# Every other residual add of an entry moved from VectorE to GpSimd

## The chip, the cores and the metric

The kernel runs on one core of a Trainium2 chip. The metric is the device time of one execution in microseconds (us), the median over runs. An execution has TensorE (PE, with its weight loads PEld), VectorE (DVE), ScalarE (ACT), GpSimd (POOL), and SyncE (SP), which starts the transfers.

## The reference

A first block (gated delta rule, windowed attention, a merge) works on 512 tokens of width 1024, and two transformer layers follow. The change touches only how one sublayer hands over to the next in these layers. There the reference does the following, four times a layer:

```
f = swiglu(rmsnorm(h, g[0]), ffn_gate[i, 0], ffn_up[i, 0], ffn_down[i, 0])
h = h + MACARON * rmsnorm(f, g[1])
mix = hybrid_mixer(rmsnorm(h, g[2]), ...)
h = h + rmsnorm(mix, g[3])
...
gate = jax.nn.sigmoid(rmsnorm(h, g[6]) @ w_ple_gate[i])
h = h + rmsnorm((p[i] @ w_ple[i]) * gate, g[7])
```

That is: norm the output of one sublayer, add it to the residual `h`, norm the residual, and multiply it by the first weights of the next sublayer.

## The kernel before

The residual lies in SBUF as `[128, 8, 512]`: 8 tiles (`KD`) of 128 features by 512 tokens, float32. Products are made of split numbers: a value is a rounded part `hi` and a remainder `lo`, and `matmul3` (L224 to L229) makes three matmuls, hi by hi, lo by hi, hi by lo. Weights arrive in granules of 128x1024, of which ScalarE makes `w_hi` (L181) and VectorE `w_lo` (L189).

A sublayer ends in an `Exit`, which gathers the sum of squares of its output (GpSimd adds the squared tiles, L508; TensorE sums over features, L515 and L518; ScalarE takes the root, L481; VectorE its reciprocal, L500). The next one begins with an `Entry`, which works in two halves of 256 tokens. For each half and each tile t:

- scale (VectorE, L331): output tile times its gain times the reciprocal root, into one of four buffers
- add (VectorE, L336): the residual tile plus that buffer
- h_hi and the square (ScalarE, L357 and L360), h_hi being the residual tile times a gain, rounded
- rest (VectorE, L340): the remainder `h_lo`
- products (TensorE, L227 to L229 out of `pe_products`) for the first two weight granules, and a sum of the square (L376)

The norm's own reciprocal root is applied to the products later, so TensorE can start as soon as tile 0 has its h_lo. Each engine runs its own list in order, and semaphores join them. VectorE's list for a half is written in steps s = 0, 1, ...: scale of tile s, add of tile s - 1, rest of tile s - 3, and then what `make` puts in (a weight split, or in Ffn 0 of layer 1 the late parts of the sublayer before). TensorE goes through the tiles of half 0, then those of half 1. Ahead of each half VectorE takes the reciprocal of the sublayer before.

Each layer has four entries: Ffn 0, MixIn, Ffn 1 (after MixOut) and Ple. The first Ffn has no sublayer before it (`leave` is None) and does no scale or add. The other seven entries do both. `chain` (L582) gives every engine the lists of the sublayers one behind the other.

Of the kernel before, what the change touches and what calls it, by code (L numbers as in the profile page):

```python
# [22 lines left out]
ALU = mybir.AluOpType  # L23
# [5 lines left out]
KD = D // P  # L29
# [55 lines left out]
class Mark:  # L85


    def __init__(self, sem, base):
        self.sem, self.base = sem, base
# [214 lines left out]
def cols(half):  # L304
    return slice(half * HALF, (half + 1) * HALF)


class Entry:
# [6 lines left out]
    def __init__(self, kit, g0, gain, delta_gain, leave):  # L315
        self.kit, self.g0, self.gain, self.delta_gain, self.leave = kit, g0, gain, delta_gain, leave
        self.hi, self.lo = kit.h
        self.buf, self.sq = (kit.work[:, a:a + 2].rearrange("p a (b n) -> p (a b) n", b=2) for a in (0, 2))
        n = 2 * KD
        self.scaled, self.added = kit.mark("scaled", n if leave else 0), kit.mark("added", n if leave else 0)  # L320
        self.rounded, self.h_ready = kit.mark("rounded", n), kit.mark("h_ready", n)
        self.squared, self.summed = kit.mark("squared", n), kit.mark("summed", n)
        self.rooted, self.rstd_ready = kit.mark("rooted", 2), kit.mark("rstd_ready", 2)

    def dve_half(self, dve, half, make=None):
        kit, x, c, at = self.kit, self.kit.residual, cols(half), half * KD

        def scale(t):
            if at + t >= 4:
                dve.wait_ge(*self.added(at + t - 3))  # L330
            dve.scalar_tensor_tensor(self.buf[:, (at + t) % 4], self.leave.source(t, half), self.delta_gain(t),  # L331
                                     kit.rstd[:, c], ALU.mult, ALU.mult).then_inc(self.scaled.sem, 1)

        def add(t):
            dve.wait_ge(*self.scaled(at + t + 1))
            dve.tensor_tensor(x[:, t, c], x[:, t, c], self.buf[:, (at + t) % 4], ALU.add).then_inc(self.added.sem, 1)  # L336

        def rest(t):
            dve.wait_ge(*self.rounded(at + t + 1))
            dve.scalar_tensor_tensor(self.lo[:, t, c], x[:, t, c], self.gain(t), self.hi[:, t, c].bitcast(F32), ALU.mult,  # L340
                                     ALU.subtract).then_inc(self.h_ready.sem, 1)

        for s in range(KD + 3):
            if self.leave and s < KD:
                scale(s)
            if self.leave and 1 <= s <= KD:
                add(s - 1)
            if s >= 3:
                rest(s - 3)
            if make:  # L350
                make(s)

    def act_tile(self, act, half, t):
        x, c, n = self.kit.residual, cols(half), half * KD + t
        if self.leave:
            act.wait_ge(*self.added(n + 1))
        act.activation(self.hi[:, t, c], x[:, t, c], ACT.Copy, scale=self.gain(t)).then_inc(self.rounded.sem, 1)  # L357
        if n >= 4:
            act.wait_ge(*self.summed(n - 3))
        act.activation(self.sq[:, n % 4], x[:, t, c], ACT.Square).then_inc(self.squared.sem, 1)  # L360
# [92 lines left out]
class Exit:  # L453
# [49 lines left out]
    def pool(self, pool):  # L503
        for t in range(1, self.full):
            pool.wait_ge(*self.out_squared(t + 1))
            if t >= 2:
                pool.wait_ge(*self.out_added(t - 1))
            pool.tensor_tensor(self.total, self.total, self.sq[:, t % 2], ALU.add).then_inc(self.out_added.sem, 1)  # L508
# [19 lines left out]
class Last:  # L528
# [26 lines left out]
    def pool(self, pool):  # L555
        pass
# [25 lines left out]
def chain(kit, sublayers):  # L582

    with stage(kit) as (block, _):
        @block.sync
        def _(sp):
            for s in sublayers:
                s.sp(sp)

        @block.tensor  # L590
        def _(pe):
            for s in sublayers:
                s.pe(pe)

        @block.gpsimd
        def _(pool):
            for s in sublayers:
                s.pool(pool)

        @block.scalar  # L600
        def _(act):
            for s in sublayers:
                s.act(act)

        @block.vector
        def _(dve):
            for s in sublayers:
                s.dve(dve)
# [1453 lines left out]
class Ffn:  # L2062
# [23 lines left out]
        fetch_ahead(self.kit, sp, self.g0, self.GRANULES)  # L2086

    def pool(self, pool):
        self.exit.pool(pool)

    def pe(self, pe):
# [120 lines left out]
class MixIn:  # L2212
# [21 lines left out]
        sp.wait_ge(*self.loaded(16 * len(self.loads)))  # L2234

    def pool(self, pool):
        pass

    def pe(self, pe):
        kit, g0, h = self.kit, self.g0, self.kit.h  # L2240
# [302 lines left out]
class Ple:  # L2543
# [19 lines left out]
        fetch_ahead(self.kit, sp, self.e0, 3 + KD)  # L2563

    def pool(self, pool):
        self.exit.pool(pool)

    def pe(self, pe):
# [433 lines left out]
```

## Time and profile before

| | |
|---|---|
| median of 3 runs | 3286.45 us (3285.54 to 3293.07) |
| profiled execution, its time | 3287.4 us |
| profiled execution, its span | 3285.6 us |
| mean granted TensorE clock | 0.961 |
| TensorE, VectorE, ScalarE, GpSimd busy | 91%, 48%, 36%, 9% |

The span goes from the first to the last instruction. The granted clock is a share of TensorE's full 2.4 GHz; 0.5 is 1.2 GHz. A busy share is an average over stages in which different engines are the limit. The places around the change are short: one entry takes some 30 us.

### The profile page before, as it was taken

The numbers are of one execution on the slowest core, as the hardware profiler recorded it, in microseconds if no ns is written. First come the engines' busy times: TensorE is split into PE (matmuls) and PEld (weight loads), VectorE is DVE, ScalarE is ACT, GpSimd is POOL, SyncE is SP. The second block draws the span as 40 slices with busy tenths as digits, with TensorE's granted clock in tenths as the row PEclk, the third lists the DMA queues.
The fourth block names the chain that finished last, engine by engine and source line by source line (L and its number), as shares of the span: only waits on it lengthen the run. The fifth ranks groups of instructions, "written<-read, shape, count | busy, mean of one in ns | idle before, by whom it ended". The sixth has DMA issues, their size and how long they took to land. (4 is left out here: it accounts for less than half of the span.)

```text
span 3285.6 us, 39993 instructions
## 1 busy us (share of the span) xinstructions
PE 2989.3 (91%) x15628; PEld 2500.4 (76%) x15628; DVE 1591.2 (48%) x2721; ACT 1193.1 (36%) x2017; POOL 294.9 (9%) x273
## 2 busy tenths in 40 slices
PE   5988799887999999959899999899999778999997
PEld 2877699866778888837688888788888556888886
DVE  5725465433454434356464434654435375644336
ACT  4324544233242223136442323533223345432234
POOL 0001086600000000020000000000000010000000
PEclk8999899999999999989999999999999899999998
DMA  5220100022223332210222332233332101232321
GB/s 211 71 70 1 63 1 1 1 65 68 85 90 97 96 103 84 90 39 1 65 83 97 96 103 84 64 110 96 99 106 84 58 1 39 77 96 97 102 92 57
DMA packets 66858, 241.93 MB, mean 74 GB/s; under 512 B 7408, under 2 KB 9584, under 8 KB 66032
## 3 DMA queue, kind: packets, MB, share of 16 engines
q1 hardware_dynamic: 66672, 239.38, 22.5%
q8 instruction: 125, 2.05, 0.3%
q14 instruction: 61, 0.50, 0.1%
HBM read 236.21 MB, written 3.15 MB: 73 GB/s over the span
## 5 line engine op out<-in xcount | busy, mean ns | idle before, releaser
L227 PE MATMUL pair<-h_hi_at,w_hi_at 128*128 128x512 f32 (+1 forms) x2048 | 781.8, 382 | 45.9 <-DVE h_lo_at L340 30.6
L228 PE MATMUL pair<-h_lo_at,w_hi_at 128*128 128x512 f32 (+1 forms) x2048 | 760.6, 371 | 0.0
L229 PE MATMUL pair<-h_hi_at,w_lo_at 128*128 128x512 f32 (+1 forms) x2048 | 760.5, 371 | 0.0
L189 DVE TENSOR_TENSOR w_lo_at<-w_raw,w_hi_at 128x1024 fp32r<-128x1024 f32 x350 | 437.0, 1251 | 472.8 <-ACT w_hi_at L181 472.7
L181 ACT ACTIVATE w_hi_at<-w_raw 128x1024 fp32r<-128x1024 f32 x350 | 366.0, 1052 | 537.8 <-PE pair L229 521.6
L227 PEld LDWEIGHTS pair<-h_hi_at,w_hi_at 128*128 128x128 f32 x2048 | 389.8, 190 | 121.7 <-DVE h_lo_at L340 37.0
L228 PEld LDWEIGHTS pair<-h_lo_at,w_hi_at 128*128 128x128 f32 x2048 | 390.1, 190 | 67.2
L229 PEld LDWEIGHTS pair<-h_hi_at,w_lo_at 128*128 128x128 f32 x2048 | 390.1, 190 | 65.8
L2181 DVE TENSOR_TENSOR work_at<-pair,rstd_at 128x512 f32<-128x512 f32 (+1 forms) x184 | 122.2, 668 | 363.2 <-PE pair L229 363.1
L227 PE MATMUL pair<-a_hi_at,w_hi_at 128*128 128x512 f32 (+1 forms) x792 | 290.1, 366 | 0.0
L228 PE MATMUL pair<-a_lo_at,w_hi_at 128*128 128x512 f32 (+1 forms) x792 | 289.4, 365 | 0.0
L229 PE MATMUL pair<-a_hi_at,w_lo_at 128*128 128x512 f32 (+1 forms) x792 | 289.4, 365 | 0.0
L508 POOL TENSOR_TENSOR exit_work_at<-exit_work_at 128x512 f32<-128x512 f32 x44 | 57.9, 1315 | 2161.6 <-ACT exit_work_at L470 2161.4
L227 PE MATMUL pair<-h_hi,w_hi 128*128 128x512 f32 (+1 forms) x432 | 166.8, 386 | 28.7 <-DVE h_lo L264 21.1
L2157 ACT ACTIVATE work_at<-work_at 128x512 f32<-128x512 f32 x88 | 55.6, 632 | 334.7 <-DVE work_at L2181 334.7
L228 PEld LDWEIGHTS pair<-a_lo_at,w_hi_at 128*128 128x128 f32 x792 | 149.3, 189 | 24.5
L227 PEld LDWEIGHTS pair<-a_hi_at,w_hi_at 128*128 128x128 f32 x792 | 149.4, 189 | 24.2
L229 PEld LDWEIGHTS pair<-a_hi_at,w_lo_at 128*128 128x128 f32 x792 | 149.3, 189 | 23.9
L228 PE MATMUL pair<-h_lo,w_hi 128*128 128x512 f32 (+1 forms) x432 | 164.0, 380 | 0.0
L229 PE MATMUL pair<-h_hi,w_lo 128*128 128x512 f32 (+1 forms) x432 | 163.7, 379 | 0.0
L189 DVE TENSOR_TENSOR w_lo<-w_raw,w_hi 128x1024 fp32r<-128x1024 f32 x59 | 71.9, 1224 | 185.2 <-ACT w_hi L181 185.2
L181 ACT ACTIVATE w_hi<-w_raw 128x1024 fp32r<-128x1024 f32 x59 | 62.1, 1059 | 216.1 <-PE pair L229 195.7
(394 smaller groups left out, 4353.9 us busy)
## 6 DMA issues: line engine op xcount, KB each, us to landing
w_raw<-in_weights SPq DMA_DIRECT2D x433, 512.0 KB, 3.5
residual<-in_x SPq DMA_DIRECT2D x1, 2048.0 KB, 12.4
cos_sin_at<-rope_table SPq DMA_DIRECT2D x2, 1024.0 KB, 4.7
out<-residual SPq DMA_DIRECT2D x16, 128.0 KB, 1.7
ctx_in<-in_ctx SPq DMA_DIRECT2D x1, 1024.0 KB, 13.0
rope_table<-zb SPq DMA_DIRECT2D x1, 1024.0 KB, 4.9
mask_at<-in_layer_masks SPq DMA_DIRECT2D x2, 512.0 KB, 4.7
levels<-in_levels SPq DMA_DIRECT2D x1, 896.0 KB, 8.3
```

The costliest lines, as they stand in the source:

```text
L181: eng.activation(self.w_hi[:, g % self.split].rearrange("p k n -> p (k n)"), self.w_raw[:, slot], ACT.Copy).then_inc(self.w_hi_ready, 1)
L189: eng.tensor_tensor(self.w_lo[:, g % self.split].rearrange("p k n -> p (k n)"), self.w_raw[:, g % RAW], self.w_hi[:, g % self.split].rearr ...
L227: pe.matmul(out, sh, mh, start=start, stop=False)
L228: pe.matmul(out, sh, ml, start=False, stop=False)
L229: return pe.matmul(out, sl, mh, start=False, stop=stop)
L508: pool.tensor_tensor(self.total, self.total, self.sq[:, t % 2], ALU.add).then_inc(self.out_added.sem, 1)
L2157: act.activation(self.gate[:, f % 2], self.gate[:, f % 2], ACT.Silu).then_inc(self.gate_silu.sem, 1)
L2181: last = dve.tensor_tensor(dst[:, f % 2, c], bank, kit.rstd[:, c], ALU.mult)
```

## The change

Adds of even tiles stay on VectorE. Adds of odd tiles go to GpSimd, whose list gets an entry's adds ahead of its exit's. The one semaphore `added` becomes two, one for each engine. Tile n is ready when the semaphore n % 2 has counted n // 2 + 1, so `added(n)` now takes the number of a tile where it took a count. What is computed stays the same. The entry of Ffn, MixIn and Ple is changed; `Last`, the final adds, is not.

```diff
-        self.scaled, self.added = kit.mark("scaled", n if leave else 0), kit.mark("added", n if leave else 0)
+        self.scaled = kit.mark("scaled", n if leave else 0)
+        self.added_by = [kit.mark(x, KD if leave else 0) for x in ("added_by_dve", "added_by_pool")]
...
+    def added(self, n):
+
+        return self.added_by[n % 2](n // 2 + 1)
+
+    def add(self, eng, half, t):
+        x, c, n = self.kit.residual, cols(half), half * KD + t
+        eng.wait_ge(*self.scaled(n + 1))
+        eng.tensor_tensor(x[:, t, c], x[:, t, c], self.buf[:, n % 4], ALU.add).then_inc(self.added_by[n % 2].sem, 1)
+
+    def pool(self, pool):
+        if self.leave:
+            for half in range(2):
+                for t in range(1, KD, 2):
+                    self.add(pool, half, t)
+
     def dve_half(self, dve, half, make=None):
...
             if at + t >= 4:
-                dve.wait_ge(*self.added(at + t - 3))
+                dve.wait_ge(*self.added(at + t - 4))
...
-        def add(t):
-            dve.wait_ge(*self.scaled(at + t + 1))
-            dve.tensor_tensor(x[:, t, c], x[:, t, c], self.buf[:, (at + t) % 4], ALU.add).then_inc(self.added.sem, 1)
...
             if self.leave and 1 <= s <= KD:
-                add(s - 1)
+                if s % 2:
+                    self.add(dve, half, s - 1)
...
     def act_tile(self, act, half, t):
...
-            act.wait_ge(*self.added(n + 1))
+            act.wait_ge(*self.added(n))
...
     def pool(self, pool):
+        self.entry.pool(pool)
         self.exit.pool(pool)
```

The last edit stands in Ffn and Ple; in MixIn, which has no exit of its own, `pass` becomes `self.entry.pool(pool)`.

## Rows read from the trace of the kernel before

**Rows 1.** The page's busy time, share of the span and instructions.
```profile
PE 2989.3 (91%) x15628; PEld 2500.4 (76%) x15628; DVE 1591.2 (48%) x2721; ACT 1193.1 (36%) x2017; POOL 294.9 (9%) x273
L227 PE MATMUL pair<-h_hi_at,w_hi_at 128*128 128x512 f32 (+1 forms) x2048 | 781.8, 382 | 45.9 <-DVE h_lo_at L340 30.6
```

**Rows 2.** Timeline of TensorE: start, duration, instruction, idle before and releaser.
```profile
2837.36 0.39 PE L227 MATMUL pair<-h_hi_at,w_hi_at 128*128 128x256 f32 x1 [2.15 <-DVE h_lo_at L340]
...
2841.86 0.43 PE L227 MATMUL pair<-h_hi_at,w_hi_at 128*128 128x256 f32 x1
...
2822.91 0.39 PE L227 MATMUL pair<-h_hi_at,w_hi_at 128*128 128x256 f32 x1 [3.31 <-DVE h_lo_at L340]
...
1295.56 0.39 PE L227 MATMUL pair<-h_hi_at,w_hi_at 128*128 128x256 f32 x1 [0.50 <-DVE h_lo_at L340]
...
2111.91 0.39 PE L227 MATMUL pair<-h_hi_at,w_hi_at 128*128 128x256 f32 x1 [2.19 <-DVE h_lo_at L340]
...
2037.02 0.38 PE L227 MATMUL pair<-h_hi_at,w_hi_at 128*128 128x256 f32 x1 [1.65 <-DVE w_lo_at L189]
```

**Rows 3.** One line's instructions, L336: duration min/median/max ns, first and last start.
```profile
L336 DVE TENSOR_TENSOR residual<-residual,work_at x112: 411/420/426, 1292.1 to 3223.5; 128x256 f32<-128x256 f32 x112
```

**Rows 4.** Timeline of VectorE in half 1 of Ffn 1, layer 1.
```profile
2834.23 0.88 DVE L331 SCALAR_TENSOR_TENSOR work_at<-delta_at,small,rstd_at 128x256 f32<-128x256 f32 x2
2835.03 0.42 DVE L336 TENSOR_TENSOR residual<-residual,work_at 128x256 f32<-128x256 f32 x1
2835.36 0.48 DVE L331 SCALAR_TENSOR_TENSOR work_at<-delta_at,small,rstd_at 128x256 f32<-128x256 f32 x1
2835.76 0.42 DVE L336 TENSOR_TENSOR residual<-residual,work_at 128x256 f32<-128x256 f32 x1
...
2836.83 0.48 DVE L340 SCALAR_TENSOR_TENSOR h_lo_at<-residual,small,h_hi_at 128x256 fp32r<-128x256 f32 x1
...
2841.33 0.48 DVE L340 SCALAR_TENSOR_TENSOR h_lo_at<-residual,small,h_hi_at 128x256 fp32r<-128x256 f32 x1
```

**Rows 5.** Timeline of the rope stage, and L2200, a 128x512 VectorE multiply elsewhere.
```profile
1443.99 1.27 POOL L1174 TENSOR_TENSOR by_cos_at<-qh_at,cos_sin_at 128x512 f32<-128x512 f32 x1 [0.63 <-DVE k_rope_at L1197]
...
1444.55 1.26 DVE L1197 TENSOR_TENSOR qh_at<-by_cos_at,by_sin_at 128x512 f32<-128x512 f32 x1
...
L2200 DVE TENSOR_TENSOR work_at<-work_at x88: 692/693/693, 955.5 to 3076.5; 128x512 f32<-128x512 f32 x88
```

**Rows 6.** Timeline at the end of Ple, layer 1.
```profile
3259.64 0.41 DVE L2691 TENSOR_TENSOR delta_at<-emb_at,sig_at 128x256 f32<-128x256 f32 x1
3259.76 1.45 POOL L508 TENSOR_TENSOR exit_work_at<-exit_work_at 128x512 f32<-128x512 f32 x1
...
3260.21 1.28 DVE L2691 TENSOR_TENSOR delta_at<-emb_at,sig_at 128x256 f32<-128x256 f32 x1 [0.15 <-ACT sig_at L2675]
```

**Rows 7.** Timeline in the delta rule's inversion stage.
```profile
429.74 0.43 DVE L1637 TENSOR_SCALAR inv_a<-inv_low 128x512 f32<-128x512 f32 x1
429.77 1.53 POOL L1721 TENSOR_TENSOR inv_b<-inv_a,levels 128x512 f32<-128x512 f32 x1
...
430.08 1.50 DVE L1638 TENSOR_SCALAR inv_low<-inv_low 128x512 f32<-128x512 f32 x1
```

**Rows 8.** Small and one-sided GpSimd instructions, by line.
```profile
L1310 POOL COPY scores<-small x32: 185/185/187, 263.2 to 343.9; 128x1 f32<-128x1 f32 x32
...
L879 POOL MEMSET c_wide<- x1: 312/312/312, 0.8 to 0.8; 128x256 f32 x1
...
L1763 POOL MEMSET scan_state<- x2: 525/525/525, 607.3 to 607.8; 128x512 f32 x2
```

**Rows 9.** Stretches: length, busy time (x instructions), granted clock, DMA share, GB/s.
```profile
2822.91:2826.60 3.69, 3.69 (x15) 3.51 (x16) 3.69 (x11) 2.16 (x7) 0.00 (x0) 0.54 0.02 4
...
2111.91:2122.94 11.03, 10.88 (x64) 10.14 (x65) 6.15 (x16) 4.90 (x13) 0.00 (x0) 0.85 0.00 0
1308.40:1317.87 9.47, 9.31 (x65) 8.57 (x65) 6.06 (x16) 5.05 (x13) 0.00 (x0) 1.00 0.00 0
```

More of the change, by code:

```diff
@@ L2236, in pool @@
     def pool(self, pool):
-        pass
+        self.entry.pool(pool)
     def pe(self, pe):
@@ L2565, in pool @@
     def pool(self, pool):
+        self.entry.pool(pool)
         self.exit.pool(pool)
```

## The prediction

> **What bounds the kernel now.** I read the page first. TensorE is busy 91% of the span, VectorE 48%, GpSimd 9% [rows 1]. So VectorE work costs time only where TensorE waits for it. The groups of instructions then say where: the idle time ahead of products of h is put down to `h_lo` of L340, the last VectorE step of an entry. The timeline shows those waits one by one [rows 2]: the reader is to see that TensorE idles 2.15 us at the start of half 1 of an entry, 3.31 us at the start of half 0 after an attention output (Ffn 1), but 0.50 us in half 0 of MixIn. In Ple it waits 1.65 us for a weight split (L189), not for h.
>
> Seven entries have a `leave`: MixIn and Ffn 1 of both layers, Ple of both, and Ffn 0 of layer 1. 112 adds of 0.42 us stand in them [rows 3], 16 an entry; 56 go to GpSimd.
>
> Then I read VectorE's order in half 1 of Ffn 1, layer 1 [rows 4]. Each instruction starts 0.08 us before the last one ends, so a scale or a rest costs 0.40 us of the stream and an add 0.34. The first rest ends at 2837.31 and TensorE starts at 2837.36 [rows 2]. The rest of tile 4 ends at 2841.81 and its products start at 2841.86: up to tile 4 TensorE runs at VectorE's pace of 1.13 us a tile. Behind that TensorE sets the pace itself.
>
> **What is taken away.** Four adds a half, 0.34 us each. Two halves of waiting would give back one add ahead of the first rest in each, 0.68 us an entry, if GpSimd's adds ran beside VectorE for nothing.
>
> **What comes in their place.** Whether they run beside each other is what decides, and three places of the trace show that they don't.
> - In the rope stage VectorE adds two SBUF tensors of 128x512 while GpSimd multiplies. GpSimd ends at 1445.26, VectorE at 1445.81, 1.26 us after its start; the same shape with GpSimd quiet takes 0.69 [rows 5]. VectorE's work began when GpSimd's was over and took 0.55 more.
> - With 128x256, our shape: GpSimd ends at 3261.21 and VectorE's multiply at 3261.49, 0.28 later, 1.28 us after its start in place of 0.41. In the same rows the first multiply ends at 3260.05, and GpSimd, which had started at 3259.76, ends 1.16 later; its instruction alone takes 1.27. So GpSimd waits too, and 0.14 us of its instruction lie ahead of the part that excludes the other engine [rows 6].
> - VectorE's next instruction doesn't get in first. At 429.74 and 430.08 two stand back to back; GpSimd starts at 429.77, ends 1.14 after the first, at 431.30, and only then does the second finish, at 431.58 [rows 7]. Whoever asks first goes first. These two read one tensor each; ours read two, as in rows 5 and 6.
>
> All VectorE instructions around the new adds (scale, add, rest) read two SBUF tensors, except the two scales that read PSUM.
>
> The Trainium skill says this too ("SBUF — State Buffer", SBUF: two separate sides): VectorE with two SBUF inputs and GpSimd reading SBUF take one port pair exclusively, the first holding it for a whole instruction. By that rule the change costs time; the rows above agree, so it is my sum and not a separate rival.
>
> **The price of a GpSimd add of 128x256.** No row has it. Two inputs at 128x512 take 1.27 us [rows 5]; a copy of one element takes 0.185 [rows 8]. Half the elements: 0.185 + (1.27 - 0.185) / 2 = 0.73 us. The memsets (0.53 for 512, 0.31 for 256) scale alike. Bounds: below, 0.31, a memset of this shape that reads nothing; above, 1.27, as if half a tile cost what a whole one does. I take 0.73, since every pair of sizes here scales so, and 0.59 of it excludes VectorE. The VectorE instruction behind it then ends 0.28 (an add) or 0.34 (scale, rest: 0.48 against 0.42) later. One collision thus puts 0.59 + 0.34 - 0.40 = 0.53 us into the stream, for an add that took 0.34.
>
> The Trainium skill ("GPSIMD Engine Reference", Performance versus the Vector engine) gives 4.50 us for a float add of 2048 elements. In proportion that is an estimate of 0.56 us for 256; with it the sum below would be about 3 us in place of 8.
>
> **One half, step by step** (half 1 of Ffn 1, from [rows 4]). The second scale ends at 2835.11; GpSimd's add of tile 1 starts 0.08 later, at 2835.19, as in rows 5, and asks at 2835.33. VectorE's add of tile 0 ends at 2835.45, so GpSimd ends at 2836.04 and scale 2 (started 2835.37) at 2836.38. Scale 3 ends 2836.78, add 2 at 2837.12. GpSimd's add of tile 3 asks at 2837.00, ahead of rest 0 (started 2837.04, asks about 2837.18), and ends at 2837.71; rest 0 ends at 2838.05, not 2837.31: 0.74 late. Two collisions, one add saved. Rest 1 has another add saved and is 0.42 late. Each further pair of tiles has one collision and one saved add. Rest 4 has four collisions against three saved adds: 4 x 0.53 - 3 x 0.34 = 1.10; followed out to the instruction it is 1.18. Since TensorE takes tile 4 as soon as it is ready, half 1 ends 1.18 us late.
>
> In half 0 it depends on the entry. Ffn 1 starts from idle: TensorE is 0.74 late at tile 0 and keeps it, since at nearly half clock [rows 9] its products are then slower than VectorE's pace. In MixIn it is TensorE again from tile 2, so rest 1's 0.42 stays (the weight split behind add 0 collides as scale 2 does). In Ffn 0 of layer 1 two VectorE instructions that read PSUM follow add 0 (L2684); GpSimd's first add runs beside them, and one collision less one add, 0.2, stays. Everything between the halves hangs on TensorE's sum through ScalarE's root, so half 1 starts late by the same.
>
> ScalarE's waits cost nothing: GpSimd's tile 1 is ready at 2836.04, before ScalarE has done with tile 0. The scales' waits for `added(n-4)` are long met. GpSimd's queue holds only the adds of the exits, which end before the entry's first scale or begin after its last tile.
>
> Sum: MixIn 2 x (0.42 + 1.18) = 3.2; Ffn 1 2 x (0.74 + 1.18) = 3.8; Ffn 0 0.2 + 0.74 = 0.9 (its half 1 is already slow by the clock, next part, so only the first wait counts); Ple 2 x 0.2 = 0.4, since its half 0 lies beside other products. Together 8.3 us.
>
> **The clock.** Half 1 of Ffn 0 takes 11.03 us at a mean granted clock of 0.85, half 1 of MixIn 9.47 at 1.00 [rows 9]. Both began after nearly the same idle, 2.19 and 2.16. So these waits stand at the edge: four of five kept 2.4 GHz, while the 3.31 us ahead of Ffn 1's half 0 was followed by 0.54, nearly all at 1.2 GHz [rows 9], and even the 1.65 in Ple has such a stretch behind it. The change lengthens the wait of 2.15 to 2.15 + 0.74 = 2.9. I take it that three of the four fall. Each costs 11.03 - 9.47 = 1.56, less the 1.18 - 0.74 = 0.44 by which VectorE's delay then hides behind the slower products: 1.1 us, together 3.4.
>
> 8.3 + 3.4 = 11.7. The profiled execution took 3287.4 (span 3285.6), 0.95 over the median of 3286.45; from the median that gives 3298.
>
> **The rivals.** A measurement here tells a change from none at about 0.3%, 9.9 us.
> - A, the forecast: exclusion and most waits over the clock's edge, +11.7, 3298. Chance 0.42.
> - B, exclusion, the clock holds: +8.3, 3294.8, within 0.3%. For it: four of five waits held so far. Against it: 2.9 is much nearer to 3.31. 0.30.
> - C, GpSimd's adds run beside VectorE: 0.68 us back in each of the five entries, -3.4, 3283. This is the one on the other side. It decides where a collision costs less than 0.34 us, a GpSimd add under 0.54. Against it all of rows 5 to 7. 0.08.
> - D, a GpSimd half tile costs nearly a whole one: each collision 1.08 us, rest 4 late by 3.3, an entry by about 5; with five, +25, 3311. Against it the memsets. 0.12.
> - E, VectorE's next instruction always goes first: one collision fewer ahead of each rest, 0.2 and 0.6 an entry, +4, 3290. Against it rows 7. 0.08.
>
> Range 3289 to 3305: it takes in A, B and E, and part of the way to D. Slower by over 0.3%: A and D, less those of A in which only one or two waits fall, 0.50. Within 0.3%: B, C, E and that part, 0.46. Faster, 0.04.
>
> **What would show it.** Right: GpSimd adds recorded at 0.73 to 0.9 us; scales and rests behind them at 0.9 to 1.1 in place of 0.48; TensorE's wait ahead of half 1 near 2.9; the granted clock of more half 1 stretches below 1. Wrong: rests that keep 0.48 (C), waits of 2.9 with the clock at 1.00 (B), GpSimd adds above 1.2 (D).

## The result and the profile after

| | before | after |
|---|---|---|
| median of 21 runs each, us | 3287.59 (3285.34 to 3293.29) | 3295.79 (3293.30 to 3299.64) |
| profiled execution, us | 3287.4 | 3294.15 |
| its span, us | 3285.6 | 3292.4 |
| mean granted TensorE clock | 0.961 | 0.960 |

The ratio is 1.0023, with a 95% interval of 1.0016 to 1.0030: slower beyond its interval, by less than the 0.3% named in the prediction. The medians are 8.2 us apart, the profiled spans 6.8. The kernel before is here 1.1 us above the 3286.45 from which the forecast was counted, so 8.2 is to be compared with its +11.7.

The page's busy times and the group of TensorE that waits for `h_lo` (us busy, mean ns | idle before; L352 is the rest, which was L340):

```profile
PE 2992.8 (91%) x15628; PEld 2503.3 (76%) x15628; DVE 1600.0 (49%) x2665; ACT 1191.2 (36%) x2017; POOL 342.0 (10%) x329
...
L227 PE MATMUL pair<-h_hi_at,w_hi_at 128*128 128x512 f32 (+1 forms) x2048 | 782.7, 382 | 50.7 <-DVE h_lo_at L352 36.4
```

Beside [rows 1], VectorE does 56 instructions fewer and is busy 9 us longer. The idle time put down to `h_lo` has grown from 30.6 to 36.4 us. The adds themselves, one line for both engines (ns, shortest/median/longest):

```profile
L333 DVE TENSOR_TENSOR residual<-residual,work_at x56: 407/414/422, 1291.3 to 3229.9; 128x256 f32<-128x256 f32 x56
L333 POOL TENSOR_TENSOR residual<-residual,work_at x56: 833/846/858, 1291.4 to 3230.1; 128x256 f32<-128x256 f32 x56
```

Now half 1 of Ffn 1, layer 1, the stretch of [rows 4]. First VectorE's timeline (start, duration, instruction), then GpSimd's and TensorE's in the same stretch. The third row is a pair of scales, and the fourth repeats the second of that pair, from a narrower window.

```profile
2840.51 0.88 DVE L347 SCALAR_TENSOR_TENSOR work_at<-delta_at,small,rstd_at 128x256 f32<-128x256 f32 x2
2841.31 0.42 DVE L333 TENSOR_TENSOR residual<-residual,work_at 128x256 f32<-128x256 f32 x1
2841.65 1.34 DVE L347 SCALAR_TENSOR_TENSOR work_at<-delta_at,small,rstd_at 128x256 f32<-128x256 f32 x2
2842.51 0.47 DVE L347 SCALAR_TENSOR_TENSOR work_at<-delta_at,small,rstd_at 128x256 f32<-128x256 f32 x1
2842.91 0.41 DVE L333 TENSOR_TENSOR residual<-residual,work_at 128x256 f32<-128x256 f32 x1
2843.24 0.94 DVE L352 SCALAR_TENSOR_TENSOR h_lo_at<-residual,small,h_hi_at 128x256 fp32r<-128x256 f32 x1
...
2848.03 0.95 DVE L352 SCALAR_TENSOR_TENSOR h_lo_at<-residual,small,h_hi_at 128x256 fp32r<-128x256 f32 x1
```

```profile
2841.47 0.83 POOL L333 TENSOR_TENSOR residual<-residual,work_at 128x256 f32<-128x256 f32 x1 [7.66 <-DVE work_at L347]
2843.07 0.84 POOL L333 TENSOR_TENSOR residual<-residual,work_at 128x256 f32<-128x256 f32 x1 [0.76 <-DVE work_at L347]
```

```profile
2844.24 0.38 PE L227 MATMUL pair<-h_hi_at,w_hi_at 128*128 128x256 f32 x1 [2.76 <-DVE h_lo_at L352]
```

What to see: VectorE's add ends at 2841.73. GpSimd's add, started at 2841.47, ends 0.58 us behind it, at 2842.31 (the rows cut thousandths off). VectorE's next scale starts at 2841.65 and ends 0.28 behind GpSimd, at 2842.59 (the pair's 1.34 us less the second scale's own part): 0.94 us for an instruction that takes 0.48 in [rows 4]. The rest meets GpSimd's second add in the same way and takes 0.94. Such a meeting is called a collision below. All 56 adds of GpSimd end 0.58 to 0.60 us (median 0.59) behind the VectorE add that they met, and a scale or rest that has waited for one ends 0.28 behind it. In one place nothing has to wait: behind VectorE's first add in Ffn 0 of layer 1 stand two VectorE instructions that read PSUM (L2684 before), and they keep their 0.75 us beside GpSimd's add:

```profile
2097.01 0.75 DVE L2699 TENSOR_TENSOR sig_at<-pair,rstd_at 128x256 f32<-128x256 f32 x2
```

```profile
2096.84 0.84 POOL L333 TENSOR_TENSOR residual<-residual,work_at 128x256 f32<-128x256 f32 x1 [5.70 <-DVE work_at L347]
```

Back in Ffn 1, it is 3.67 us from the first scale's start to the end of rest 0 where [rows 4] has 3.08, so rest 0 is 0.59 late and TensorE waits 2.76 in place of 2.15 [rows 2]. Rest 4 ends 8.47 after the first scale in place of 7.58: 0.89 late.

The same differences, read for each entry, with the time at which half 1's reciprocal root comes and the end of the entry, both against before and from the entry's first scale on (the rests of half 1 from its own reciprocal on):

| entry | rest 0 late, half 0 | half 1's reciprocal late | rest 0, rest 4 late, half 1 | end of entry late |
|---|---|---|---|---|
| MixIn, layer 0 and 1 | 0.68 | 0.34, 0.36 | 0.60, 0.88 | 2.29, 1.88 |
| Ffn 1, layer 0 and 1 | 0.60 | 0.45, 0.41 | 0.60, 0.89 | 1.31, 1.28 |
| Ffn 0, layer 1 | 0.13 | 1.10 | 0.60, 0.88 | 0.38 |
| Ple, layer 0 and 1 | 0.70 | 0.03, 0.02 | 0.59, 0.88; 0.23, 0.52 | 0.03, -0.37 |

The ends add to 6.80 us, the difference between the spans. Outside the entries the differences cancel (0.8 us earlier ahead of the first, 0.9 later between MixIn and Ffn 1 of layer 0, 0.1 earlier later on).

MixIn's first rest is 0.68 late and not 0.60 because its first collision falls on the weight split of L189, which takes 1.76 us in place of 1.22. One number of the table is not the change's: the 1.10 of Ffn 0. Its rests 1 to 4 of half 0 are not late at all. TensorE ran its half 0 at 1.2 GHz for longer, 5.7 us in place of 3.6 behind its first product, and the kernels half1_only and early_half1 below, whose half 0 is that of before, show 1.13 and 1.08 at the same place.

The clock in the stretches of half 1, in the order MixIn 0, Ffn 1 of layer 0, Ffn 0, MixIn 1, Ffn 1 of layer 1 (length, TensorE busy, granted clock, DMA share, GB/s):

```profile
1308.53:1319.35 10.82, 10.82 (x64) 0.84 0.00 0
1663.21:1672.93 9.72, 9.52 (x64) 1.00 0.01 2
2117.34:2127.05 9.71, 9.51 (x64) 1.00 0.00 0
2491.60:2501.98 10.38, 10.38 (x64) 0.86 0.00 0
2844.24:2853.95 9.71, 9.50 (x64) 1.00 0.01 2
```

Both MixIn stretches, which had 1.00 before, contain a part at 1.2 GHz. Both of Ffn 1 do not, behind the same wait. Ffn 0's, the one at 0.85 in [rows 9], is now at 1.00, though its wait grew from 2.19 to 2.79:

```profile
2117.34 0.39 PE L227 MATMUL pair<-h_hi_at,w_hi_at 128*128 128x256 f32 x1 [2.79 <-DVE h_lo_at L352]
...
2491.60 0.58 PE L227 MATMUL pair<-h_hi_at,w_hi_at 128*128 128x256 f32 x1 [2.76 <-DVE h_lo_at L352]
```

### The profile page after: what moved, and what is told of

It is laid out like the page before. It is cut to its first block and busy times, and to the rows that moved or that the text cites. A ratio compares the mean times of both kernels' runs of the same rounds, so it can differ in the third digit from the quotient of the medians.

```text
span 3292.4 us, 39993 instructions
## 1 busy us (share of the span) xinstructions
PE 2992.8 (91%) x15628; PEld 2503.3 (76%) x15628; DVE 1600.0 (49%) x2665; ACT 1191.2 (36%) x2017; POOL 342.0 (10%) x329
## 5 line engine op out<-in xcount | busy, mean ns | idle before, releaser
L227 PE MATMUL pair<-h_hi_at,w_hi_at 128*128 128x512 f32 (+1 forms) x2048 | 782.7, 382 | 50.7 <-DVE h_lo_at L352 36.4
L189 DVE TENSOR_TENSOR w_lo_at<-w_raw,w_hi_at 128x1024 fp32r<-128x1024 f32 x350 | 439.2, 1257 | 471.7 <-ACT w_hi_at L181 471.6
L189 DVE TENSOR_TENSOR w_lo<-w_raw,w_hi 128x1024 fp32r<-128x1024 f32 x59 | 71.9, 1224 | 184.7 <-ACT w_hi L181 184.6
```

Of the source, the lines that this page charges most:

```text
L189: eng.tensor_tensor(self.w_lo[:, g % self.split].rearrange("p k n -> p (k n)"), self.w_raw[:, g % RAW], self.w_hi[:, g % self.split].rearr ...
L227: pe.matmul(out, sh, mh, start=start, stop=False)
```

## The experiments

Ratios are to the kernel before, timed on the same chip, with 95% intervals; "late" is against the profiled execution of before, in half 1 from its own reciprocal on. In the first four, VectorE keeps all 16 adds of an entry, and GpSimd in addition works on spare tiles at the moments at which the change would have it add: work that nothing reads.

**beside_add: the added cost alone, nothing taken from VectorE**

```diff
+    def pool(self, pool):
+        if self.leave:
+            for n in range(1, 2 * KD, 2):
+                pool.wait_ge(*self.scaled(n + 1))
+                pool.wait_ge(*self.beside(n // 2))
+                pool.tensor_tensor(self.kit.squares[:, 5:7], self.kit.squares[:, 7:9], self.kit.squares[:, 0:2], ALU.add).then_inc(self.beside.sem, 1)
```

> All residual adds stay on VectorE, as in the kernel before. GpSimd, at the moments at which the change has it add a tile, adds two constant 128x256 tiles into a place that nobody reads, and no engine waits for it. Theory 1 (exclusion: the two engines take turns): the changed kernel showed its first rest 0.60 us late with two collisions and one add saved, so a collision is (0.60 + 0.34) / 2 = 0.47 us; with no add saved the first rest of half 1 is 0.94 late, the rest of tile 4 is 1.9 late, MixIn and Ffn 1 lose 2.8 us each, Ffn 0 2.3, together +13 us (3300), and a scale behind such an add takes 0.95 us in place of 0.48. Theory 2 (the cost is that GpSimd hands its tiles over late): nobody waits for these adds, so no rest is late and the time stays at the 3287 of before.

3307.95 us (4 executions), ratio 1.0056 (1.0041 to 1.0071). VectorE in half 1 of Ffn 1, layer 1, then GpSimd:

```profile
2854.68 0.88 DVE L339 SCALAR_TENSOR_TENSOR work_at<-delta_at,small,rstd_at 128x256 f32<-128x256 f32 x2
2855.47 0.42 DVE L344 TENSOR_TENSOR residual<-residual,work_at 128x256 f32<-128x256 f32 x1
2855.81 0.95 DVE L339 SCALAR_TENSOR_TENSOR work_at<-delta_at,small,rstd_at 128x256 f32<-128x256 f32 x1
...
2857.74 0.95 DVE L348 SCALAR_TENSOR_TENSOR h_lo_at<-residual,small,h_hi_at 128x256 fp32r<-128x256 f32 x1
```

```profile
2855.64 0.84 POOL L331 TENSOR_TENSOR squares<-squares 128x256 f32<-128x256 f32 x1 [7.67 <-DVE work_at L339]
2857.57 0.84 POOL L331 TENSOR_TENSOR squares<-squares 128x256 f32<-128x256 f32 x1 [1.09 <-DVE work_at L339]
```

Two VectorE instructions ahead of the end of rest 0 take 0.95 in place of 0.48, and that rest is 0.94 late: two collisions of 0.47. Rest 4, behind four, is 1.88 late, 0.47 each. With the change's saved adds (0.34 each) taken off, 2 x 0.47 - 0.34 = 0.60 and 4 x 0.47 - 3 x 0.34 = 0.86, against 0.59 to 0.60 and 0.88 to 0.89 in the change. The addends are constants in tiles of their own, so it is neither the data nor the residual that VectorE waits for. The rests came as Theory 1 has them, the time did not: its sum was +13 us, and the medians are 19.7 apart. The other 6.7 are not shown to be exclusion (in the profiled execution 3.5 had arisen ahead of the first entry, where the kernels don't differ).

**beside_memset: the same moments, an instruction that reads nothing** (the edit is to beside_add)

```diff
-                pool.tensor_tensor(self.kit.squares[:, 5:7], self.kit.squares[:, 7:9], self.kit.squares[:, 0:2], ALU.add)...
+                pool.memset(self.kit.squares[:, 5:7], 0.0)...
```

> As beside_add, but GpSimd's instruction is a memset of 128x256, which reads nothing. Theory 1a (only a GpSimd instruction that reads SBUF excludes VectorE): rests not late, +0 us. Theory 1b (any GpSimd instruction does): a memset of 0.31 us less 0.14 ahead and 0.07 of slack costs 0.10 us a collision, the rest of tile 4 is 0.4 late, +3 us. Theory 2: +0 us.

3294.57 us, ratio 1.0011 (1.0001 to 1.0020). No rest 0 to 4 of any half is late, counted from the half's own reciprocal, and the scales keep their time:

```profile
L331 POOL MEMSET squares<- x56: 311/311/315, 1292.8 to 3230.3; 128x256 f32 x56
...
L339 DVE SCALAR_TENSOR_TENSOR work_at<-delta_at,small,rstd_at x96: 476/482/493, 1291.9 to 3228.7; 128x256 f32<-128x256 f32 x96
```

So the price is not that of GpSimd having something to do, nor of its semaphores. But the time is longer, and the trace puts part of that on the clock. Two stretches, the first and the second MixIn, behind waits of 2.15 us as before:

```profile
1309.00:1318.47 9.47, 9.31 (x65) 1.00 0.00 0
2490.89:2501.97 11.08, 10.92 (x65) 0.85 0.00 0
```

```profile
2490.89 0.39 PE L227 MATMUL pair<-h_hi_at,w_hi_at 128*128 128x256 f32 x1 [2.15 <-DVE h_lo_at L348]
```

The second holds a part at 1.2 GHz and is 1.61 us longer. Half 1 of Ffn 1, layer 0, did the same (its entry ends 2.13 late), and some 4 us of the span's 7.5 arose outside the entries. It bears on every comparison here: two kernels that wait equally long can differ by several us. Why this one is above before in ten executions, and not only in the profiled one, stays open.

**beside_copy and beside_add128: one input (the edit is to beside_memset), and half the size**

```diff
-                pool.memset(self.kit.squares[:, 5:7], 0.0)...
+                pool.tensor_copy(self.kit.squares[:, 5:7], self.kit.squares[:, 7:9])...
```

> As beside_add, but GpSimd copies one 128x256 tile, so it reads one tensor. Theory 1 (one input is enough): a copy of about 0.45 us costs some 0.25 us a collision, the rest of tile 4 is 1.0 late, about +6 us. If only two inputs on both sides exclude: +0. Theory 2: +0.

3296.82 us, ratio 1.0025 (1.0015 to 1.0034).

```profile
L331 POOL COPY squares<-squares x56: 526/533/538, 1294.5 to 3233.4; 128x256 f32<-128x256 f32 x56
```

Rest 0 of half 1 is 0.27 late, rest 4 0.55: 0.14 a collision. The copy takes 0.53 us with its wait, so it costs VectorE less than the 0.25 that I expected; by the medians the kernel is 8.6 us above before all the same, where I expected 6.

The second is beside_add with one tile of 128x128 in place of each 128x256:

```diff
-                pool.tensor_tensor(self.kit.squares[:, 5:7], self.kit.squares[:, 7:9], self.kit.squares[:, 0:2], ALU.add)...
+                pool.tensor_tensor(self.kit.squares[:, 5:6], self.kit.squares[:, 7:8], self.kit.squares[:, 0:1], ALU.add)...
```

> As beside_add with half the width: GpSimd adds two constant 128x128 tiles that nobody waits for. It settles how the price of a collision goes with size. By the line through 0.185 us (one element) and 1.27 us (512) the add takes 0.46 us, excludes VectorE for 0.32, and a collision costs 0.32 + 0.30 - 0.40 = 0.22 us, so the first rest of half 1 is 0.44 late. If the price belongs to the instruction and not its size: 0.94 late as in beside_add. If GpSimd's overhead lies inside the exclusion: about 0.6 late.

A single execution, 3301.19 us.

```profile
L331 POOL TENSOR_TENSOR squares<-squares x56: 565/570/583, 1294.7 to 3237.3; 128x128 f32<-128x128 f32 x56
```

Rest 0 is 0.40 late, rest 4 0.80: 0.20 a collision. With 0.47 at 128x256, half the work on GpSimd costs VectorE 0.27 less. VectorE's own instructions kept their size, so 0.20 and 0.47 differ by GpSimd's half tile alone. It ends 0.32 us behind VectorE's add, as the line through 0.185 and 1.27 has it.

**half1_only, half0_only: the change in one half of each entry**

```diff
+        self.on_pool = [n for n in range(n) if n % 2 and n >= KD]
+        self.on_dve = [n for n in range(2 * KD) if n not in self.on_pool]
...
-                if s % 2:
+                if at + s - 1 in self.on_dve:
                     self.add(dve, half, s - 1)
```

(the diff is to the changed kernel; half0_only has `n < KD`)

> The change in half 1 alone; half 0 keeps all its adds on VectorE. Theory 1: half 0 as before, in half 1 the first rest 0.60 late and the rest of tile 4 0.88, so 0.9 us in each of the five entries where TensorE waits, +4.4 us, and some more where the wait of 2.76 in place of 2.15 makes the clock fall (1.1 and 0.7 us in the two entries in which it fell in the changed kernel). Theory 3 (the changed kernel's cost comes from half 0, and half 1 only inherits it): +0.

> The change in half 0 alone. Theory 1 (a collision costs 0.47 us, a saved add gives 0.34): rest 0 of half 0 is 0.6 late, rest 1 0.27; MixIn carries 0.34 into half 1, Ffn 1 0.4 to 0.6, Ple and Ffn 0 nothing; the wait ahead of half 1 keeps its 2.15 us, and half 1 its length. Together +1.5 to +2 us without the clock, less than a comparison can tell. Theory 3 (the changed kernel's cost comes from half 0): +7.

half1_only: 3294.38 us, ratio 1.0018 (1.0008 to 1.0027). Half 0 is unchanged to 0.01 us up to rest 4; in half 1 rest 0 is 0.60 late and rest 4 0.89, and TensorE waits 2.75 to 2.80. The stretches of half 1 of both MixIn and of Ffn 1, layer 0, hold parts at 1.2 GHz.

half0_only: 3292.54 us, ratio 1.0009 (1.0000 to 1.0018). Rest 0 of half 0 is 0.60 late in Ffn 1 and 0.68 in MixIn, half 1's reciprocal 0.35 late in MixIn and 0.59 and 0.46 in Ffn 1; behind it half 1 is unchanged, with waits of 2.15. Still both MixIn stretches fell, again behind unlengthened waits.

The delays of the rests are those of the whole change, half by half. The times, 0.18% and 0.09% against 0.23% for the whole, agree within their intervals, which are as wide as the smaller part. Ffn 1's reciprocal shows less than it seems: in layer 0 it is 0.35 late in half1_only, whose half 0 is that of before, and 0.94 in beside_memset, where no rest up to tile 4 is late.

**last_only: only tile 7 of each half goes to GpSimd**

```diff
-        self.on_pool = [n for n in range(n) if n % 2 and n >= KD]
+        self.on_pool = [n for n in range(n) if n % KD == 7]
```

> GpSimd adds only tile 7 of each half, the one tile whose add comes after the wait is over. Theory 1: its collision falls ahead of rest 4, which is 0.47 late, while the saved add shows from rest 5 on (0.13 late). So TensorE loses 0.47 in half 1 of the five entries, +2.3 us without the clock. If an add could be moved for nothing once TensorE has its first tile: -0 to -1 us.

3294.40 us, ratio 1.0017 (1.0008 to 1.0026). Rests 0 to 3 are unchanged. Rest 4, which meets the one GpSimd add, is 0.47 late; rest 5, with its saved add, 0.14. Tile 7 is the only add of a half that lies behind all scales and the first rests, and it gains nothing: the price shows on the rest that it meets. In the MixIn of layer 0 the entry ends 0.42 late. MixIn 1 and both Ffn 1 fell in clock, with waits of 2.15 to 2.16 ahead of them, and ended 1.61 to 2.15 late. By the medians it is 5.8 us above before, where the sum without the clock was 2.3.

**early_half1, early_both: VectorE keeps the adds, the rest of a tile comes one step earlier**

If a first rest that is late by 0.6 costs time, one that is early by the same reasoning gives some back. The second scale-and-add pair ahead of rest 0 needs no second engine to get out of its way: rest 0 can stand ahead of it.

```diff
-    def dve_half(self, dve, half, make=None):
+    def dve_half(self, dve, half, make=None, lag=3):
...
-            if s >= 3:
-                rest(s - 3)
+            if lag <= s < KD + lag:
+                rest(s - lag)
...
-        self.dve_half(dve, 1)
+        self.dve_half(dve, 1, lag=2)
```

early_both does it in half 0 too, unless the sublayer before is Ple, and ScalarE takes the earlier sublayer's squares one tile sooner:

```diff
-                if half == 0 and t == 3 and leave:
+                if half == 0 and leave and t == (3 if isinstance(leave, GatedExit) else 2):
                     leave.act_squares(act, 1)
...
-        self.dve_half(dve, 0, make)
+        self.dve_half(dve, 0, make, lag=3 if isinstance(leave, GatedExit) else 2)
```

> All adds on VectorE as before, but in half 1 VectorE does the rest of tile s - 2 in step s in place of s - 3, so that one scale and one add fewer stand ahead of the first rest. If VectorE's order ahead of the first rest is what TensorE waits for, every rest of half 1 up to tile 4 ends 0.73 us earlier, the wait of 2.15 becomes 1.42, and five entries give 3.7 us; the clock may give 1.1 to 1.6 more in the entry where half 1 ran slow. -3.7 to -5. If ScalarE's h_hi is the limit (0.51 us after add 0): nothing.

> As early_half1, and in half 0 too (not where the sublayer before is Ple), with ScalarE's squares of the last output tile one tile earlier, since adds of tile 2 on then come 0.40 later and TensorE's sum would wait for them. Half 0 of MixIn and Ffn 1 gives another 0.73 each: -6.6 us without the clock, 3280 beside a before of 3287. If only one half's wait can be shortened because the other takes it up: no more than early_half1.

> The same kernel as early_both, beside early_both_split on one chip: a ratio to before of 0.9976 within its interval again, and a profiled execution that shows whether the stretches at 1.2 GHz stay at the same entries (they fell in MixIn and Ffn 1 of layer 0) or move from execution to execution.

| | median, us | ratio (interval) |
|---|---|---|
| early_half1 | 3283.68 | 0.9984 (0.9975 to 0.9993) |
| early_both | 3281.25 | 0.9976 (0.9967 to 0.9985) |
| early_both_again, the same kernel | 3281.90 | 0.9982 (0.9973 to 0.9991) |

By the medians these are 4.9, 7.4 and 6.1 us under before, where 3.7 and 6.6 were the sums without the clock; the second comparison bears the first out.

early_both in half 1 of Ffn 1, layer 1; VectorE, then TensorE:

```profile
2837.64 0.42 DVE L336 TENSOR_TENSOR residual<-residual,work_at 128x256 f32<-128x256 f32 x1
2837.98 0.48 DVE L331 SCALAR_TENSOR_TENSOR work_at<-delta_at,small,rstd_at 128x256 f32<-128x256 f32 x1
2838.37 0.42 DVE L336 TENSOR_TENSOR residual<-residual,work_at 128x256 f32<-128x256 f32 x1
2838.71 0.48 DVE L340 SCALAR_TENSOR_TENSOR h_lo_at<-residual,small,h_hi_at 128x256 fp32r<-128x256 f32 x1
```

```profile
2839.24 0.39 PE L227 MATMUL pair<-h_hi_at,w_hi_at 128*128 128x256 f32 x1 [1.76 <-DVE h_lo_at L340]
```

In the halves that these kernels change, MixIn's and both Ffn's, each rest up to tile 4 comes 0.73 earlier, one scale and one add. (Ple's rests kept their times.) TensorE waits 1.43 in early_half1 and 1.76 in early_both, where half 0 is early as well. There rest 7 of MixIn's half 0, and with it half 1's reciprocal, comes 0.40 earlier and not 0.73: behind the weight split of step 8 one rest stands where two did.

**early_both_split: that weight split one step sooner**

```diff
-            if s == KD:
+            if s == (KD if isinstance(leave, GatedExit) else KD - 1):
```

> early_both gave half 0 its rests 0.73 us earlier but passed only 0.40 of it on to half 1: the weight split of L189, put in at step 8, now stood behind rest 6 in place of rest 5, and so waited for one more h_hi of ScalarE. Here it goes in at step 7, behind rest 5 as before. If that is the cause, the reciprocal of half 1 starts 0.73 earlier than in the kernel before in MixIn, in place of 0.40, and likewise in Ffn 1 unless the clock differs: 0.33 us in each of four entries, 1.3 us under early_both, about 3280 beside a before of 3288. If the 0.33 is lost elsewhere: as early_both.

3284.20 us, ratio 0.9988 (0.9979 to 0.9998), where early_both_again on the same chip has 0.9982: no gain. The reciprocal of MixIn came 0.14 and 0.12 earlier than before and not 0.73, so later than in early_both: my expectation failed by its sign. VectorE at the end of half 0 of MixIn, layer 0, then ScalarE:

```profile
1302.76 0.49 DVE L340 SCALAR_TENSOR_TENSOR h_lo_at<-residual,small,h_hi_at 128x256 fp32r<-128x256 f32 x1 [0.41 <-ACT h_hi_at L357]
1303.17 1.22 DVE L189 TENSOR_TENSOR w_lo_at<-w_raw,w_hi_at 128x1024 fp32r<-128x1024 f32 x1
1304.30 0.42 DVE L336 TENSOR_TENSOR residual<-residual,work_at 128x256 f32<-128x256 f32 x1
1304.64 0.48 DVE L340 SCALAR_TENSOR_TENSOR h_lo_at<-residual,small,h_hi_at 128x256 fp32r<-128x256 f32 x1
1305.30 0.48 DVE L340 SCALAR_TENSOR_TENSOR h_lo_at<-residual,small,h_hi_at 128x256 fp32r<-128x256 f32 x1 [0.18 <-ACT h_hi_at L357]
```

```profile
1304.75 0.51 ACT L357 ACTIVATE h_hi_at<-residual,small 128x256 fp32r<-128x256 f32 x1 [1.01 <-DVE residual L336]
```

At the end of step 7 the split lies ahead of the add of tile 7, not only of rests. ScalarE waits for that add 1.01 us, and rest 7 comes 0.14 earlier than in the kernel before, where early_both has 0.40. I had looked at what the split does to rest 7 and not at what else stands behind it.

**early_both_pool: the change, on top of early_both**

```diff
             if self.leave and 1 <= s <= KD:
-                add(s - 1)
+                if s % 2:
+                    self.add(dve, half, s - 1)
             if lag <= s < KD + lag:
                 rest(s - lag)
```

> The change on top of early_both. A collision of 0.47 us against a saved add of 0.34: rest 0 is 0.13 later than in early_both, rest 1 0.60, rest 3 0.73, so half 1 of the five entries loses about 0.7 and half 0 0.3 to 0.6: +4 to +5 us over early_both, 3286. If the earlier rest gives GpSimd's adds a place beside VectorE: no slower than early_both, 3281.

3293.33 us, ratio 1.0014 (1.0005 to 1.0024), where early_both has 0.9976: all of its gain is gone. In half 1 the rests 0 to 3 are 0.60, 0.12 and 0.46 us earlier and 0.03 later than before; early_both has 0.73 earlier for each. The change thus makes them 0.13, 0.61, 0.27 and 0.76 later, as expected for rests 0, 1 and 3: rest 0 now has one collision ahead of its end and one add less (0.47 - 0.34 = 0.13). I expected 4 to 5 us over early_both without the clock; the kernels' medians, of different comparisons, are 12 apart, so the time missed by 7. The mean granted clock of the profiled executions is 0.957, against 0.959 and 0.962 of early_both; the remainder may lie there, which no run isolates.

## Why the prediction came out as it did

**What bounds the kernel** held. What differs outside the seven entries cancels, and inside them the time is lost ahead of products of h or by the clock in them.

**Exclusion** held, and beside_add and beside_memset show it as the cause: an add beside VectorE's two-input instructions costs, a memset of the same shape at the same moments does not. The Trainium skill ("SBUF — State Buffer", SBUF: two separate sides) says that a VectorE instruction with two SBUF inputs and a GpSimd instruction that reads SBUF exclude each other; the trace agrees, with 0.95 in place of 0.48 us beside an add, and 0.482 beside a memset, which reads nothing.

**First come, first served** held too: in every pair of the after rows the engine that asked first ends first, and rival E (one collision fewer ahead of each rest) would have given rest 0 a lateness of 0.2 where 0.60 was measured. That VectorE instructions which read PSUM run beside GpSimd was right as well: rest 0 of Ffn 0 is 0.13 late.

**The collision** was forecast at 0.59 + 0.34 - 0.40 = 0.53 us and is 0.59 + 0.28 - 0.40 = 0.47. GpSimd's part was right: it ends 0.59 us behind VectorE's instruction, as forecast. The other term was mis-sized: the VectorE instruction that has waited ends 0.28 behind GpSimd, where I took 0.34 for a scale or rest. By that rest 0 of half 1 is 0.60 late and not 0.74, rest 4 0.88 and not 1.18. GpSimd's add of 128x256 comes out at 0.14 + 0.59 = 0.73 us, if the 0.14 ahead of the exclusive part holds at this size; no run has this add without a wait. The 0.14 itself was read from the wrong pair: 1.27 less 1.16 is 0.11, but the instruction of [rows 6] is L508, of whose 44 in the trace of before 40 take 1.29 to 1.30 us, and 1.30 less 1.16 is 0.14. The Trainium skill's figure ("GPSIMD Engine Reference", Performance versus the Vector engine), taken in proportion, was an estimate of 0.56 us. The trace does not bear it out at this size: the part behind VectorE's add alone is 0.59, and the measurement decides.

**The saved adds** were right: 0.34 us each, seen in rest 1 and in last_only's rest 5 (0.47 - 0.34 = 0.13, measured 0.14).

**Half 0.** MixIn's reciprocal was forecast 0.42 late and is 0.34 to 0.36, in half0_only too, and at most 0.02 in half1_only, whose half 0 is that of before. Ffn 1's was forecast 0.74 late, the full lateness of tile 0; tile 0 is 0.60 late, and 0.41 to 0.45 arrive; since 0.35 and 0.94 arrive in layer 0 of half1_only and beside_memset, whose first rests there are not late, no run shows how much of it is the change's. Ple costs 0.02 to 0.03 instead of 0.2.

**The sum without the clock** was 8.3 us. From the table, with 0.87 us for half 1 behind its reciprocal (both Ffn 1, and rest 4): MixIn 2 x (0.35 + 0.87) = 2.4; Ffn 1 2 x (0.43 + 0.87) = 2.6; Ffn 0 0.13 + 0.60 = 0.7; Ple 0.05. Together 5.8 us.

**The clock** is the step that failed: its condition (an edge of the wait) and its net size, 1.0 us where 3.4 stood. I took it that three of four waits, lengthened past an edge, would be followed by 1.2 GHz, at 1.1 us each. In the profiled execution two were, at 2.29 - 0.34 - 0.87 = 1.08 and 1.88 - 0.36 - 0.87 = 0.65 us, together 1.7. But Ffn 0's stretch, behind a wait that grew to 2.79, went the other way (1.32 us shorter in half 1, 0.97 longer in half 0), and it and Ple give back 0.7: 1.0 net, and 5.8 + 1.0 = 6.8. Nor is there an edge. The prediction's own 1.65 in Ple, with 1.2 GHz behind it, spoke against one. Of the four half 1 stretches of MixIn and Ffn 1, so many hold a part at 1.2 GHz, from one profiled execution of each kernel:

| wait ahead of half 1, us | stretches of 4 |
|---|---|
| 1.43 | early_half1 0 |
| 1.72 to 1.76 | early_both 2, early_both_again 0, early_both_split 0 |
| 1.87 | early_both_pool 2 |
| 2.15 | before 0, beside_memset 2, half0_only 2, last_only 3 |
| 2.43 to 2.56 | beside_copy 2, beside_add128 3 |
| 2.76 | after 2, half1_only 3 |
| 3.10 | beside_add 3 |

Longer waits are followed by 1.2 GHz more often, but at one wait the count goes from 0 to 3, and one kernel, early_both, shows 2 in one execution and 0 in another. My count for after was near; my count for before, 0 at 2.15, was that of one execution and is the lowest of its row. So the step counted as the change's doing what at 2.15 happens too. What decides it within a row stays open. It also limits the account of the medians: 5.8 us of the 8.2 between them are counted from instructions (0.9 of it Ffn 1's half 0, which is not sure to be the change's), and the other 2.4 cannot be told from differences of clock, of which beside_memset has more with no rest late at all. Every kernel with more GpSimd work in the entries lies further above before than its late rests: 6.3 us for 0 in beside_memset, 6.1 for 4.4 in half1_only, 3.9 for 1.5 to 2 in half0_only. Whether that is the clock alone, no run isolates.

**The outcome** is 3295.79, +8.2 for a forecast of +11.7. The direction was right and the time lies in the range; the likeliest number was 2 us too high by itself and 3.5 as a difference, the rest being that before was slower in this comparison. "Slower by over 0.3%", which had 0.50, did not come; "within 0.3%", with 0.46, did. By size the outcome is rival B's (+8.3), and that is luck: B's own sum was 2.5 too large, and what fills the gap is in no sum of B's. C would have shown scales of 0.48 beside GpSimd's adds, D adds above 1.2 us; neither appears.

## What to carry to other kernels

An add that is moved to GpSimd is not taken off VectorE when both work on SBUF tensors: a two-input GpSimd instruction of 128x256 float32 delays VectorE's next two-input instruction by 0.47 us here, more than the 0.34 that the add had cost there. Count collisions ahead of the instruction that the bound engine waits for, each at its price, against the instructions saved; the same rests came 0.73 us earlier simply by reordering VectorE's own list (in both halves 0.9976 of the time before, and 0.9982 in a second comparison, the best version here). When the effect looked for is a few us in 3290, read the instructions' starts entry by entry, since kernels with equal waits differ by as much through the clock.

## What the runs showed of the hardware

- VectorE's delay falls faster than GpSimd's size: 0.47 us for an add of 128x256, 0.20 for half of it, 128x128 (GpSimd's own 0.85 and 0.57, waits included), 0.14 for a copy of 128x256, 0 for a memset of it.
- VectorE instructions of 128x256 that read PSUM and one SBUF tensor kept their time beside a GpSimd add: a pair took 0.75 us with and without it. One place shows this.
- GpSimd pays as well: its 56 adds take 0.846 us at the median, of which, by the collisions above, some 0.12 is waiting (an estimate: 0.85 less 0.73).
- One kind of stretch, MixIn's half 1 behind a wait of 2.15 us, took 9.47 us in one place and 11.08 in another of the same execution (beside_memset), at granted clocks of 1.00 and 0.85, while Ffn 0's behind 2.79 had 1.00 in the changed kernel.
